# ScalarE scales taps of a long convolution for GpSimd, which takes four channel tiles instead of three; the last inner feed-forward slabs get buffers of their own

## The reference

```python
def swiglu_ffn(x, w_in, w_out):
    gate, up = jnp.split(x @ w_in, 2, axis=-1)
    return (jax.nn.silu(gate) * up) @ w_out          # 2816 hidden

# token_mixer, h is (256, 1024)
z = h @ w_in
u_glu, q_lat, kv_lat, k_r, gate_logits = jnp.split(z, IN_SPLIT, axis=-1)
ua, ub = jnp.split(u_glu, 2, axis=-1)
u = ua * jax.nn.sigmoid(ub)
u = causal_depthwise_conv_2(u, conv_w, conv_b)       # 31 taps, 1024 channels
u = jax.nn.silu(layer_norm(u, conv_norm_g, conv_norm_b))
y_a = u @ w_conv_out
q = (rms_norm(q_lat, q_norm_g) @ w_uq)               # 8 heads
kv = (rms_norm(kv_lat, kv_norm_g) @ w_ukv)
o = mla_attention(q_nope, q_rope, k_nope, k_rope, v)
y_b = o @ w_attn_out
y = (g_a * y_a + g_b * y_b) @ w_out

y = jnp.square(jax.nn.relu(h @ w_mlp_in)) @ w_mlp_out  # 4096 hidden
```

## Time and profile before

| | before |
|---|---|
| median of 3 runs | 1086.38 us |
| profiled execution: its time | 1085.63 us |
| profiled execution: its span, first to last instruction | 1083.8 us |
| mean granted TensorE clock | 0.979 |
| TensorE busy | 1054.2 us, 97% |
| DVE busy | 811.8 us, 75% |
| ScalarE busy | 478.1 us, 44% |
| GpSimd busy | 498.3 us, 46% |
| HBM | 187.10 MB read, 174 GB/s over the span |

### The profile page before, as it was taken

The page is one execution under the profiler, slowest core; times in us unless marked ns, Lnnn a source line. Parts: engine busy times, 40 slices in busy tenths (PEclk is TensorE's granted clock), DMA queues, the critical chain, the costliest instruction groups (busy, mean ns, idle before and its releaser), DMA issues.

```text
span 1083.8 us, 20035 instructions
## 1 busy us (share of the span) xinstructions
PE 1054.2 (97%) x8257; PEld 1019.2 (94%) x8257; DVE 811.8 (75%) x827; ACT 478.1 (44%) x527; POOL 498.3 (46%) x310
## 2 busy tenths in 40 slices
PE   9999999999989999999999999999799999999998
PEld 8999999998989899999999999978699989999998
DVE  5877676789867468878776769999878678667753
ACT  6433434566521354434344434554466363343341
POOL 4557575300051007667678899998600004314400
PEclk9999999999999999999999999997799999999998
DMA  9977777454330157586866455562134527675631
GB/s 276 315 235 249 235 241 245 145 161 149 118 117 0 58 186 229 194 261 203 266 204 227 124 149 175 139 203 68 50 114 134 187 73 233 211 243 170 228 117 40
DMA packets 165997, 188.86 MB, mean 174 GB/s; under 512 B 10574, under 2 KB 155548, under 8 KB 165820
## 3 DMA queue, kind: packets, MB, share of 16 engines
q1 hardware_dynamic: 165580, 186.13, 53.8%
q0 software_dynamic: 192, 1.88, 0.4%
q10 hardware_dynamic: 176, 0.14, 0.1%
HBM read 187.10 MB, written 1.05 MB: 174 GB/s over the span
## 4 chain that ended last, share of the span: by engine, by line
PE 82%; DVE 13%; ACT 3%; issue 1%; DMA 1%; ACTq 0%; SPq 0%; DVEq 0%
PE ps L1788 49%; PE ps L1821 18%; DVE ps L1518 4%; PE ps L1987 4%; DVE wl L1159 3%; ACT wh L746 1%; PE ps L1911 1%; PE ps L1971 1%; PE ps L1852 1%; PE ps L1963 1%; PE ps L1835 1%; PE ps L1860 1%; PE ps L2332 1%; DMA raw<-in_w_ukv 1%; PE ps L1842 0%
## 5 line engine op out<-in xcount | busy, mean ns | idle before, releaser
L1788 PE MATMUL ps<-xh,wh 128*128 128x256 f32 x1256 | 362.2, 288 | 1.0 <-DVE xl L1709 0.8
L1788 PE MATMUL ps<-xl,wh 128*128 128x256 f32 x1256 | 358.1, 285 | 0.0
L1788 PE MATMUL ps<-xh,wl 128*128 128x256 f32 x1256 | 357.9, 285 | 0.0
L1164 DVE TENSOR_TENSOR wl<-raw,wh 128x2048 fp32r<-128x2048 f32 x78 | 248.1, 3180 | 61.2 <-ACT wh L752 61.2
L1788 PEld LDWEIGHTS ps<-xh,wh 128*128 128x128 f32 x1256 | 243.7, 194 | 6.0 <-issue 5.4
L1788 PEld LDWEIGHTS ps<-xl,wh 128*128 128x128 f32 x1256 | 243.8, 194 | 0.2
L1788 PEld LDWEIGHTS ps<-xh,wl 128*128 128x128 f32 x1256 | 243.7, 194 | 0.0
L752 ACT ACTIVATE wh<-raw 128x2048 fp32r<-128x2048 f32 x84 | 160.5, 1911 | 163.4 <-PE ps L1788 163.4
L625 POOL TENSOR_TENSOR ada_raw<-ada_raw,c_act 128x2048 f32<-128x2048 f32 x24 | 89.5, 3730 | 305.9 <-DMA ada_raw<-in_w_ada 300.8
L1159 DVE TENSOR_TENSOR wl<-raw,wh 128x2048 fp32r<-128x2048 f32 (+1 forms) x74 | 181.9, 2467 | 38.7 <-ACT wh L746 34.6
L746 ACT ACTIVATE wh<-raw 128x2048 fp32r<-128x2048 f32 (+2 forms) x68 | 127.6, 1878 | 102.8 <-PE ps L1788 85.1
(11 more groups left out here) (361 smaller groups left out, 1625.5 us busy)
## 6 DMA issues: line engine op xcount, KB each, us to landing
raw<-in_ffn_w_in SPq DMA_DIRECT2D x43, 1024.0 KB, 7.4
ada_raw<-in_w_ada SPq DMA_DIRECT2D x24, 1024.0 KB, 5.3
raw<-in_ffn_w_out SPq DMA_DIRECT2D x22, 1024.0 KB, 4.9
raw<-in_w_in SPq DMA_DIRECT2D x18, 1024.0 KB, 5.5
raw<-in_w_mlp_in SPq DMA_DIRECT2D x16, 1024.0 KB, 5.6
raw<-in_w_mlp_out SPq DMA_DIRECT2D x16, 1024.0 KB, 5.0
raw<-in_w_mix_in SPq DMA_DIRECT2D x14, 1024.0 KB, 5.3
raw<-in_w_mix_out SPq DMA_DIRECT2D x4, 1024.0 KB, 5.2
```

Source lines behind the costliest of these rows:

```text
L1164: dve.tensor_tensor(wl[:, s % SLOTS, :], raw[:, s % SLOTS, :], wh[:, s % SLOTS, :].bitcast(F32), ALU.subtract).then_inc(low_done, 1)
L1788: mm = pe.matmul(bank[:, m * T:(m + 1) * T], w[:, k, m * P:(m + 1) * P], r[:, k, :], start=(m == 0 and k == 0 and j == 0), stop=(k == KT - ...
```

## The change

- GpSimd gets the tiles (0, 1) and (6, 7), DVE keeps (2, 3) and (4, 5), so DVE has 62 pairs of taps where it had 62 and 31 single ones.
- For taps whose number isn't a multiple of three (k below 31 of the first pair of tiles, below 22 of the second: 20 + 14) ScalarE makes the two products, into one of two buffers in turn (`tap_mem`), and GpSimd only adds them. The others GpSimd does alone, through `tap_own`. ScalarE waits with tap n until sum n-2 is done (`tap_added`), GpSimd with a sum until its products are there (`tap_scaled`).
- ScalarE's scalings stand at fixed places of its queue (`scale_taps`): four behind the first pair of `glu`, two or four at each further one, two ahead of the cast at each `lat`, two behind the lat roots, two ahead of the casts of `uq` 0 and 1 and of both `ukv`, two ahead of `gate_b` 3, the last two behind the first exponential of attention.
- DVE's portions become 1 at each `uq` (3 before), none at `ukv`, 5 at each of heads 0 to 6.
- In the feed-forward blocks and the MLP the last hidden tile is written to `last_high` and `last_low`, parts of buffers that are free then. ScalarE's rounding of it no longer waits for the down slab before, and in the feed-forward blocks it is ahead of two casts; DVE does the last product and `rest` ahead of the split of slab s+4.
- The semaphores of q, k and v become one, in the same order.

```diff
-POOL_TILES = ((0, 1), (7,))
-DVE_TILES = ((2, 3), (4, 5), (6,))
+POOL_TILES = ((0, 1), (6, 7))
+DVE_TILES = ((2, 3), (4, 5))
+ACT_TAPS = [(n, k) for n, last in ((0, TAPS), (1, 22)) for k in range(1, last) if k % 3]
...
+    "head_parts": (("q", 6), ("k", 4), ("v", 4)),
...
-        tap_mem = tiles(pt_mem[:, 6 * P:6 * P + 2 * T], 2)
+        tap_mem = [tiles(pt_mem[:, 6 * P + n * 2 * T:6 * P + (n + 1) * 2 * T], 2) for n in range(2)]
+        tap_own = tiles(con[:, N_CONST_BOTH + KT * T:N_CONST_BOTH + KT * T + 2 * T], 2)
...
+        last_high = {"ffn1": yl[:, 4:6, :], "ffn2": xh[:, 0:2, :], "mlp": xh[:, 0:2, :]}
+        last_low = {"ffn1": yl[:, 6:8, :], "ffn2": xl[:, 0:2, :], "mlp": xl[:, 0:2, :]}
...
+                for k in range(1, TAPS):
+                    if (g, k) in ACT_TAPS:
+                        n = ACT_TAPS.index((g, k))
+                        pool.wait_ge(*at("tap_scaled", n + 1))
+                        pool.tensor_tensor(sums, sums, tap_mem[n % 2], ALU.add).then_inc(S("tap_added"), 1)
+                        pool.wait_ge(*at("tap_added", n + 1))
+                        continue
                     for n, t in enumerate(group):
...
+                        ins = pool.tensor_scalar(tap_own[:, n, :], upad[:, t, k:k + T], tap(k, t), 0.0, ALU.mult, ALU.add)
                     ps_(ins)
                     ps_.sync()
...
+                    ins = pool.tensor_tensor(sums, sums, tap_own, ALU.add)
...
-                with act.Fori(0, FF_STEPS - 1) as i:
+                with act.Fori(0, FF_STEPS - 2) as i:
...
+                s = s0 + 3 * FF_STEPS - 4
+                cast(s + 3)
+                silu(FF_STEPS)
+                round_hidden(FF_STEPS, last_high[name])
+                cast(s + 4)
+                cast(s + 5)
...
+            taps_ahead = list(range(len(ACT_TAPS)))
+
+            def scale_taps(count):
+                for _ in range(count):
+                    n = taps_ahead.pop(0)
+                    g, k = ACT_TAPS[n]
+                    act.wait_ge(*at("glu", POOL_TILES[g][-1] // 2 + 1))
+                    if n >= 2:
+                        act.wait_ge(*at("tap_added", n - 1))
+                    for j, t in enumerate(POOL_TILES[g]):
+                        ins = act.activation(tap_mem[n % 2][:, j, :], upad[:, t, k:k + T], ACT.Copy, scale=tap(k, t))
+                    ins.then_inc(S("tap_scaled"), 1)
+
             for n in range(4):
                 s = FIRST["glu"] + 2 * n
+                if n > 1:
+                    scale_taps(2)
                 cast(s + 3)
+                if n:
+                    scale_taps(2)
...
                 cast(s + 4)
+                if n == 0:
+                    scale_taps(4)
...
             for n in range(3):
+                scale_taps(2)
                 cast(s + n + 3)
...
+            scale_taps(2)
             for t in range(5):
                 act.wait_ge(*at("lat_n", 1))
...
+                if n < 2:
+                    scale_taps(2)
                 cast(s + 3)
...
+            scale_taps(2)
             gate_logits("gate_b", 3, ps[3])
             attn_exp(0)
+            scale_taps(len(taps_ahead))
...
-                act.wait_ge(taken, s + 2)
-                square(k + 1)
+                if k < MLP_STEPS - 1:
+                    act.wait_ge(taken, s + 2)
+                    square(k + 1)
+                else:
+                    square(k + 1, last_high["mlp"])
...
-                sub(s + 4)
-                hidden(FF_STEPS)
-                rest(FF_STEPS)
+                hidden(FF_STEPS)
+                rest(FF_STEPS, last_high[name], last_low[name])
+                sub(s + 4)
...
-                convolve(3)
+                convolve(1)
             sub(FIRST["ukv"] + 3)
-            convolve(3)
...
-                    convolve(7 if h in GATE_AT_HEAD else 6)
+                    convolve(5)
```

More of the change, by code:

```diff
@@ L781, in silu, with round_hidden @@
                     act.activation(hid[:, 1, :], hid[:, 0, :], ACT.Silu).then_inc(S(name + "_silu"), 1)
-                def round_hidden(count):
+                def round_hidden(count, high=fh):
                     act.wait_ge(*at(name + "_h", count))
-                    act.activation(fh[:, :, :], pair(hid[:, 3, :]), ACT.Copy).then_inc(S(name + "_fh"), 1)
+                    act.activation(high[:, :, :], pair(hid[:, 3, :]), ACT.Copy).then_inc(S(name + "_fh"), 1)
                 cast(s0 + 3)
@@ L1119, in _, with square @@
             s0 = FIRST["mlp_in"]
-            def square(count):
+            def square(count, high=fh):
                 act.wait_ge(*at("mlp_relu", count))
-                act.activation(fh[:, :, :], pair(hid[:, 0, :]), ACT.Square).then_inc(S("mlp_fh"), 1)
+                act.activation(high[:, :, :], pair(hid[:, 0, :]), ACT.Square).then_inc(S("mlp_fh"), 1)
             cast(s0 + 3)
@@ L1216, in hidden, with rest @@
                     dve.tensor_tensor(hid[:, 3, :], hid[:, 1, :], hid[:, 2, :], ALU.mult).then_inc(S(name + "_h"), 1)
-                def rest(count):
+                def rest(count, high=fh, low=fl):
                     dve.wait_ge(*at(name + "_fh", count))
-                    dve.tensor_tensor(fl[:, :, :], pair(hid[:, 3, :]), fh[:, :, :].bitcast(F32), ALU.subtract)\
+                    dve.tensor_tensor(low[:, :, :], pair(hid[:, 3, :]), high[:, :, :].bitcast(F32), ALU.subtract)\
                         .then_inc(S(name + "_fl"), 1)
@@ L1722, in rest @@
                 dve.wait_ge(*at("mlp_fh", count))
-                dve.tensor_tensor(fl[:, :, :], pair(hid[:, 1, :]), fh[:, :, :].bitcast(F32), ALU.subtract)\
+                dve.tensor_tensor(low[:, :, :], pair(hid[:, 1, :]), high[:, :, :].bitcast(F32), ALU.subtract)\
                     .then_inc(S("mlp_fl"), 1)
```

36 lines of the change are left out of this document (19 added, 17 removed).

## The result

The changed kernel takes 1088.7 us (median of 20 runs, 1086.5 to 1091.9), the kernel before 1085.3 beside it: a ratio of 1.0041, 95% interval 1.0031 to 1.0051. By that ratio it is slower by 4.4 us; the two medians lie 3.4 us apart. The forecast had the sign and the mechanism, but about twice the size: 8.6 us. The profiled execution took 1090.99 us, its span 1089.2; it is 2.3 us above the median of its own kernel.

The account below looks back on a forecast made before the run. TensorE, busy 97% of the span, was taken as the bound. From the profiled 1085.63: - 4.0 (last slabs) + 17.0 (ring) - 4.4 (attention) = 1094.2, plus 0.75 to the median: 1095.0 us, range 1080 to 1104.

Parts of the forecast that it names:

- the last inner slabs: Last down slabs of feed-forward blocks and MLP: own buffers remove TensorE's waits, 2.5 + 1.5 = 4.0 us gained.
- ScalarE's wait: Convolution before attention: two buffers make ScalarE wait for GpSimd's sums, holding casts, then splits, then TensorE; 17 us lost.
- The 2 us per split: Convolution stretch: each DVE weight-slab split costs GpSimd about 2 us.
- the ring: Two buffers of scaled taps, convolution to attention: ScalarE's waits make the cast before attention late by 17 us.
- The first point: Third lat step: GpSimd adds index 17 at 684, lat square done at 688.6 us, TensorE 11.7 us late.
- The second point: Cast before attention (724.89 us before): GpSimd adds index 29 at 741, cast comes at 742, late by 17.
- the lower bound of this term: Cast before attention: late by at least 12 us, if GpSimd doesn't idle and meets fewer splits.
- attention: From DVE's first score work to the convolution's mean: 58.2 us instead of 62.6, 4.4 us gained, 7.0 with clock high.
- The low clock: Attention's last gate slab: TensorE idles about 5 us before it, so it takes 8.5 us instead of 5.8.
- Half-paid: Rival: only the 12 us at the lat square are late, attention gives 7.0; 1087.4 us, chance 0.13.
- The faster case: Rival: the two buffers never hold ScalarE, a split costing GpSimd at most 0.6 us; 1078.0 or 1075.4 us, chance 0.20.
- The lower clock: Rival: waits in lat and gate slabs lower TensorE's clock, 2.7 us a slab; three give 1103 us, chance 0.14.

Follow-up runs that it names:

- e11: The changed kernel as it is, run again beside e12 on one chip: 1087.8 us, ratio 1.0037 to the kernel before.
- e1: The kernel before with only the last inner slabs' buffers and their order, convolution unchanged: 1081.8 us, ratio 0.998 to the kernel before.
- e3: The changed kernel, ScalarE never waiting for sums and GpSimd adding its own buffer instead of the scaled taps: 1079.6 us, ratio 0.9952 to the kernel before.
- e5: The changed kernel with twelve DVE splits made on 2 columns instead of 2048: 1080.3 us, ratio 0.9967 to the kernel before.
- e6: The changed kernel with attention's two maxima going through PSUM: 1088.8 us, ratio 1.0046 to the kernel before.
- e12: The changed kernel with maxima through PSUM, run again beside e11 on one chip: 1087.8 us, ratio 1.0044 to the kernel before.
- e9: The changed kernel, scalings placed by e7's trace where ScalarE idles and the buffer is free: 1077.5 us, ratio 0.9932 to the kernel before.
- e7: The changed kernel with 10 scaled taps of the first pair, 18 of the second, 14 of these in attention: 1090.4 us, ratio 1.0061 to the kernel before.
- e4: The changed kernel with four buffers for scaled taps up to tap 25, then two: 1086.4 us, ratio 1.0015 to the kernel before.
- e8: The changed kernel with e7's plan and the maxima through PSUM: 1090.1 us, ratio 1.0058 to the kernel before.
- e10: The changed kernel with e9's plan and the maxima through PSUM: 1075.3 us, ratio 0.9917 to the kernel before.

## Why the prediction was right and wrong, step by step

**Right: what bounds, and where it can be lost.** Attention, the last slabs and the stretch from 617 us to attention are where the change moves the offsets. Two more places move by over 1 us, both with the clock: 260 to 271 us (1.6 lost, not in e11), and the last matmuls (1.3 gained; 0.72 over the last 6.2 us, 0.50 over the last 7.8 before).

**Right: the last inner slabs, 4.0 us.** The waits for `fl` are gone from TensorE's list, 1.10, 1.35 and 1.51 us in the traces; across the three slabs the offsets fall by 1.2, 1.5 and 1.7 us, 4.4 in sum. That the shifted split would cost nothing held as well. In the times of e1 only 2.2 us (0.5 to 3.8) are seen, so the times leave open whether all of it arrives.

**Right: ScalarE's wait is the mechanism.** The wait for two buffers reaches the casts, from them the splits, from them TensorE. e3 takes away the wait and nothing else and gets 0.9952 for 1.0041, 9.7 us; e5 takes away the splits and leaves the wait and gets 0.9967, 8.0 us. So the way from the wait to TensorE has an experiment, e3, and the way from the splits to the wait another, e5. The steps from cast to split to TensorE are read from the traces. The 2 us per split were right also: 1.9 by the nine splits.

**Mis-sized: the ring, 17 us forecast, 10.5 measured.** This is the step that failed. It came from two fixed points, and both were placed by the wrong row.

- The first point. The work of 45.6 us and the price of 2 us a split were in the text, and so were nine splits. Their sum is 617.6 + 45.6 + 9 x 2 = 681. I wrote 684, the time at which the kernel before had done it with eleven splits, and so counted two splits that no longer stood there. Measured: 679.6. The square was then done at 684.26, where I had 688.6; TensorE was 7.5 us late instead of 11.7. Some 1.7 of these are not waits: an estimate, the 5.5 us by which the offset grows from 655 to 674 us less the wait of 3.78.
- The second point. From 684 I added 32.4 of work, 21 for nine splits and four products and 4 of idling. Measured from 679.6 to 734.0, where I had 741: 54.4 us, of which 32.4 work, 5.2 idling for tap 22 (703.27 in the trace below) and 16.8 for splits and products. The idling was right, the splits' share 4 us too large, the start another 4.4. The cast came at 734.89, late by 10.0, not 17.

```profile
696.82 1.29 POOL L734 TENSOR_TENSOR work<-work,con 128x512 f32<-128x512 f32 x1
703.27 3.71 POOL L727 TENSOR_TENSOR work<-work,ada_raw 128x512 f32<-128x512 f32 x2 [5.15 <-ACT ada_raw L980]
```

I had also given 12 us as the lower bound of this term, "if it doesn't idle and meets fewer splits". It idled and still stayed below: the bound hung on the first point, which itself was late by 4. A bound that shares an anchor with the estimate is not independent of it.

The account from trace to trace, 5.4 us where I had 8.6: the ring 10.5 (17 forecast), attention -1.5 (-4.4), the last slabs -4.4 (-4.0), and, not forecast, 1.6 at 260 to 271 us, 0.5 ahead of the first block's last slab and -1.3 at the end. The two large errors partly cancel. The other half of the way from 1095.0 to 1088.7 lies outside the kernel: I added 0.75 us because the profiled execution of the kernel before lay that much under the median of its 3 runs, and the changed kernel's lies 2.3 above its own.

**Mis-sized: attention, 4.4 us forecast, 1.5 measured** (60.80 us from the second head's scores to the mean before, 59.33 now; 58.0 in e11's profile, which would be 2.8). Counted from DVE's first score work (739.78), as the forecast was, the mean came after 60.8 us, where I had 58.2 (by its own terms 55.7 and 2.7 it should have been 58.4): a gain of 1.9. The last gate slab started at 52.2 instead of 48.9, and took 7.8 us, where I had 8.5. I had DVE through 52 us after its first score work; it was at 54.4. The difference is L1632: I took 0.17 us for it, as with GpSimd silent, and it takes 0.54 on average over the eight heads, 2.9 us more in sum. I had not asked what GpSimd, which I gave more sums, would do to DVE's small operations. But e6 and e12 show that giving it back moves no median, so L1632 explains DVE's lateness and is not shown to explain the time. The low clock was right: TensorE's granted clock over the stretch is 0.79, as in the kernel before (0.78), and the last gate slab ran in part at the low level. That it met this slab is partly luck: in e11's profile it met the slab before (8.0 us) and not this one (5.8).

```profile
741.20:800.60 59.40, 53.23 (x293) 44.09 (x294) 51.83 (x116) 26.97 (x72) 28.66 (x35) 0.79 0.22 71
```

**The rivals.** Half-paid (1087.4) came closest in time, with another sum: the ring cost 10.5 and not 12, attention gave 1.5 and not 7. The faster case's condition, a split costing GpSimd at most 0.6 us, was not met (1.9), and e5, in which the splits are all but gone, is indeed faster, 1080 us. The lower clock ahead of attention came once and for less than a slab, behind the wait of 3.78 us at 669.62, where the matmuls start every 0.21 us instead of 0.12; it is some 1.7 us and not three slabs of 2.7. The stage, with the granted clock third from the end:

```profile
666.00:674.00 8.00, 4.38 (x24) 4.41 (x25) 7.93 (x7) 5.88 (x8) 7.68 (x5) 0.79 0.41 127
```

The Trainium skill's rule (SBUF — State Buffer, Who interferes with whom), by which a DVE operation with two inputs in SBUF and a GpSimd operation that reads SBUF shut each other out for a whole instruction, agrees with the trace in the worst place: two sums of 1.29 us each took 6.67 beside two splits (5.59). On average the price is a little less than a whole split: 1.9 us, where a split beside a silent GpSimd takes 2.29 (at 776.82). That a sum already running ends first may be why; it is not shown.

## What to carry to other kernels

When an engine with time to spare gets work that others read, look at what stands behind each new wait in its own queue: here a wait of one scaling held a cast, and through it TensorE. Nearly the same work in the same two buffers (30, 34 and 28 scaled taps) gave 0.9932, 1.0041 and 1.0061 of the kernel before, depending mainly on where the scalings stand (e9, the change, e7), and the places can be read from a trace: where the helper idles, and when the consumer frees the buffer. And when work moves away from a stretch, count the interference that is left by the new order of the program; a time read from the old trace still holds the old one. The rows of e4 suggest the reverse too, untested: with a wait taken away, an engine works where it stood idle, as GpSimd does there beside DVE's latents.

## What the runs showed of the hardware that I had not expected

- A DVE operation on 2 columns with its operands in SBUF takes 0.17 us alone and up to 1.07 beside GpSimd's sums of 1.3 us, and then ends with the sum; with its input in PSUM it stays at 0.16 (e6, e8, e10, e12). What it loses is set by the sum and not by its own size.
- Once DVE's splits are gone (e5), all ten of GpSimd's pairs of sums from 618.6 to 671.6 us take 2.67 or 2.68 us, although DVE's taps, which read one operand from SBUF and one from PSUM, go on beside them (twelve in 5.46 us at 642.94).
- The time of a run goes roughly with its mean granted clock: of the kernel before, beside e11, the runs at 0.977 took 1086.0 to 1086.5 us and those at 0.983 took 1080.7 to 1082.4, but those at 0.979 lie anywhere from 1083.6 to 1088.2. Two single profiled executions can differ by over 4 us where the medians agree: e6's took 1086.30 us and the changed kernel's 1090.99, with medians of 1088.8 and 1088.7.
